# Feed-forward down projection by seven block products instead of eight in 9 of 11 units

## The chip, the core and the metric

One Trainium2 chip, one of its cores. The metric is the device time of one launch in microseconds (us), lower is better. Engines: TensorE (PE, with its weight loads as PEld), VectorE (DVE), ScalarE (ACT), GpSimd (POOL) and SyncE (SP), which issues the loads.

## The reference

Two blocks of two layers each over 256 tokens of width 1024. The first block (attention mixes and a mixture of experts) is not touched. A layer of the second block is

```
h = h + 0.5 * swiglu(rms_norm_2(h, ffn1_norm[l]), ffn1_w1[l], ffn1_w3[l], ffn1_w2[l])
h = h + token_mixer(...)
h = h + 0.5 * swiglu(rms_norm_2(h, ffn2_norm[l]), ffn2_w1[l], ffn2_w3[l], ffn2_w2[l])
swiglu(u, w1, w3, w2) = (silu(u @ w1) * (u @ w3)) @ w2      # w1, w3: 1024 x 2816, w2: 2816 x 1024
```

so there are four feed-forward parts. All data are 32-bit floats.

## The kernel before

**Products.** A 32-bit operand is split into a high part (rounded, by ScalarE) and a low part (the rest, by VectorE). `products` (L473 to L477) makes one product of a 128x128 stationary tile with a 128x512 moving tile by three matmuls: high by high (L475), high by low (L476), low by high (L477).

**A feed-forward part** is 11 units (`NU2`) of 256 hidden columns (`FE`). The tokens are two chunks of 128. A unit has three slabs of 128x2048 weights, held in a ring of three slots (`raw`, with `whi` and `wlo` for the split): two for the up and gate columns (k tiles 0 to 3 and 4 to 7) and one of `w2` for the down projection. TensorE does per unit: `unit_up`, 16 products for both chunks into banks 4 and 5; `unit_down`, 8 products (2 chunks by 2 halves of the columns by 2 k tiles) that accumulate over all units in banks 0 to 3 (`ybank`); `unit_transposes` (L903), four 128x128 transposes of the activation into bank 6. In the loop `unit_up` of unit u is followed by `unit_down` of unit u - 1 and by the transposes of unit u.

**The helpers.** ScalarE: `split_hi` of each slab in two halves (L464), silu of each chunk (L1630), `hi_part` of the transposed activation (L1640). VectorE: `split_lo` (L471), `activations` (L2058: gate times up), `lo_part` (L2063). At the end of a part `ffn_residual` adds half of each bank to x (L2466) and TensorE transposes x for the next stage (`transposes_h`, L1447) ahead of the last quarter of the last down projection; in the last part of all the final scaling follows (L2641).

**Order.** Each engine's program is written out by hand and run in order, and the engines are tied by counting semaphores: `slab_done` (TensorE is through with a slab), `hi_made` and `lo_made` (splits), `raw_in` (a load landed), `sg`, `a`, `aT`, `a_hi`, `a_lo` (the steps of the activation), `y_part`, `x_ready`. An engine that waits holds up all that is behind it on its own queue. `Fori` is a loop on the chip.

## Time and profile before

| | us |
|---|---|
| median of 3 runs (1526.9 to 1527.73) | 1527.6 |
| the profiled execution | 1526.78 |
| its span | 1525.0 |
| busy: PE / PEld / DVE / ACT / POOL | 1494.8 / 1142.2 / 828.7 / 716.2 / 98.3 |

The page gives each engine's busy time over the whole span, a strip of 40 slices, and the chain of work that ended last, of which 92% is TensorE. The four feed-forward parts lie at about 503 to 684, 825 to 1008, 1014 to 1195 and 1336 to 1515 us. The granted TensorE clock is 0.997 of full speed over the span.

### The profile page before, as it was taken

What the parts mean: (1) busy time and instruction counts of PE and PEld (TensorE: products, weight loads), DVE (VectorE), ACT (ScalarE), POOL (GpSimd) and SP (SyncE); (2) the same over time, 40 slices, a digit from 0 to 9 for tenths busy, and PEclk for the clock granted to TensorE, in tenths of its full rate; (3) what the DMA queues carried; (4) which work ended last, traced back from release to release, by engine and by line L of the source; (5) the groups of instructions that cost most, each with busy time, mean ns of one, the idle gap of its engine ahead of it and who ended that gap; (6) DMA issues with size and microseconds to landing.
All of it is one profiled execution on the core that took longest, in us unless ns stands there. A gap on an engine that the chain in (4) does not pass through costs nothing.

```text
span 1525.0 us, 20880 instructions
## 1 busy us (share of the span) xinstructions
PE 1494.8 (98%) x7748; PEld 1142.2 (75%) x7748; DVE 828.7 (54%) x1120; ACT 716.2 (47%) x1193; POOL 98.3 (6%) x166
## 2 busy tenths in 40 slices
PE   8999999999999999999999999999999999999998
PEld 7886335887433888888888888888888888888886
DVE  5675225576324655555766554565455566755544
ACT  5673223674213544445655444454444537454443
POOL 2321001231000000002000000000000100000000
PEclk9999999999999999999999999999999999999999
DMA  7739995547899555556345666656555643565551
GB/s 251 261 130 393 371 419 213 205 166 300 354 422 332 193 186 181 190 194 199 105 166 190 197 192 192 188 169 194 187 188 182 217 144 116 201 207 182 191 192 56
DMA packets 166054, 328.36 MB, mean 215 GB/s; under 512 B 8906, under 2 KB 106960, under 8 KB 153056
## 3 DMA queue, kind: packets, MB, share of 16 engines
q1 hardware_dynamic: 164992, 323.52, 60.7%
q0 software_dynamic: 992, 3.89, 0.9%
q8 instruction: 46, 0.75, 0.2%
q14 instruction: 24, 0.20, 0.0%
HBM read 326.33 MB, written 1.05 MB: 215 GB/s over the span
## 4 chain that ended last, share of the span: by engine, by line
PE 92%; DVE 3%; ACT 3%; DVEq 1%; issue 1%; DMA 1%; POOL 0%; SPq 0%; POOLq 0%; ACTq 0%
PE bank L475 24%; PE bank L477 23%; PE bank L476 23%; PE bank L1278 7%; PE bank L1327 4%; PE bank L903 1%; PE bank L1336 1%; PE bank L978 1%; DMA sb_raw<-w_in 1%; PE bank L1447 1%; PE bank L1069 1%; ACT sb_whi L464 1%; PE bank L1487 1%; PE bank L1515 0%; PE bank L1507 0%
## 5 line engine op out<-in xcount | busy, mean ns | idle before, releaser
L471 DVE TENSOR_TENSOR sb_wlo<-sb_raw,sb_whi 128x1024 fp32r<-128x1024 f32 (+1 forms) x417 | 479.9, 1194 | 321.8 <-ACT sb_whi L464 321.4
L464 ACT ACTIVATE sb_whi<-sb_raw 128x1024 fp32r<-128x1024 f32 (+2 forms) x419 | 408.1, 1028 | 295.5 <-PE bank L477 286.0
L475 PE MATMUL bank<-sb_whi,sb_op_hi 128*128 128x512 f32 (+2 forms) x1212 | 474.1, 391 | 3.4 <-DVE sb_op_lo L2089 1.7
L477 PE MATMUL bank<-sb_whi,sb_op_lo 128*128 128x512 f32 (+2 forms) x1212 | 466.3, 385 | 0.0
L476 PE MATMUL bank<-sb_wlo,sb_op_hi 128*128 128x512 f32 (+2 forms) x1212 | 465.5, 384 | 0.0
L475 PEld LDWEIGHTS bank<-sb_whi,sb_op_hi 128*128 128x128 f32 x1212 | 228.1, 188 | 49.9 <-issue 2.1
L477 PEld LDWEIGHTS bank<-sb_whi,sb_op_lo 128*128 128x128 f32 x1212 | 227.8, 188 | 45.9
L476 PEld LDWEIGHTS bank<-sb_wlo,sb_op_hi 128*128 128x128 f32 x1212 | 228.3, 188 | 42.4
L475 PE MATMUL bank<-sb_whi,sb_lat_hi 128*128 128x512 f32 (+2 forms) x456 | 175.7, 385 | 1.0 <-DVE sb_wlo L471 1.0
L477 PE MATMUL bank<-sb_whi,sb_lat_lo 128*128 128x512 f32 (+2 forms) x456 | 174.5, 383 | 0.0
L476 PE MATMUL bank<-sb_wlo,sb_lat_hi 128*128 128x512 f32 (+2 forms) x456 | 174.4, 382 | 0.0
L475 PEld LDWEIGHTS bank<-sb_whi,sb_lat_hi 128*128 128x128 f32 x456 | 85.6, 188 | 18.2 <-DVE sb_wlo L471 1.5
L477 PEld LDWEIGHTS bank<-sb_whi,sb_lat_lo 128*128 128x128 f32 x456 | 85.6, 188 | 16.3
L476 PEld LDWEIGHTS bank<-sb_wlo,sb_lat_hi 128*128 128x128 f32 x456 | 85.7, 188 | 15.9
L1630 ACT ACTIVATE sb_unit_work<-bank,sb_small 128x256 f32<-128x256 f32 x88 | 41.7, 474 | 115.8 <-PE bank L477 115.6
L2058 DVE SCALAR_TENSOR_TENSOR sb_unit_work<-bank,sb_small,sb_unit_work 128x256 f32<-128x256 f32 x88 | 42.4, 482 | 81.3 <-ACT sb_unit_work L1630 81.3
L1278 PE MATMUL bank<-sb_moe,sb_xg 128*64 128x512 f32 x288 | 70.9, 593 | 0.6 <-DVE sb_unit_work L2421 0.5
L2393 DVE TENSOR_TENSOR sb_unit_work<-bank,sb_unit_work 128x256 f32<-128x256 f32 x16 | 10.1, 631 | 100.8 <-ACT sb_unit_work L1873 100.8
L1873 ACT ACTIVATE sb_unit_work<-bank 128x256 f32<-128x256 f32 x16 | 6.1, 384 | 123.2 <-PE bank L1278 123.2
L778 POOL TENSOR_TENSOR sb_small<-sb_small,sb_half 128x2 f32<-128x2 f32 x5 | 3.5, 703 | 789.6 <-DVE sb_small L2455 789.6
L1278 PEld LDWEIGHTS bank<-sb_moe,sb_xg 128*64 128x64 f32 x288 | 22.3, 137 | 41.5 <-issue 40.0
L2063 DVE TENSOR_TENSOR sb_lat_lo<-bank,sb_lat_hi 128x512 fp32r<-128x512 f32 x44 | 30.2, 686 | 19.5 <-ACT sb_lat_hi L1640 19.5
(283 smaller groups left out, 1335.2 us busy)
## 6 DMA issues: line engine op xcount, KB each, us to landing
sb_raw<-ffn_w SPq DMA_DIRECT2D x264, 512.0 KB, 4.3
sb_raw<-w_in SPq DMA_DIRECT2D x84, 512.0 KB, 4.6
sb_moe<-exp_w_gate_up SPq DMA_DIRECT2D x36, 1024.0 KB, 11.9
sb_moe<-exp_w_down SPq DMA_DIRECT2D x18, 1024.0 KB, 11.5
sb_raw<-w_out SPq DMA_DIRECT2D x32, 512.0 KB, 4.3
sb_own<-exp_w_gate_up SPq DMA_DIRECT2D x12, 1024.0 KB, 8.5
sb_per_block<-exp_w_gate_up SPq DMA_DIRECT2D x4, 1024.0 KB, 4.9
sb_xg<-exp_w_gate_up SPq DMA_DIRECT2D x4, 1024.0 KB, 9.6
```

Of the source, the lines that this page charges most:

```text
L464: nc.scalar.activation(h, r, ACT.Copy).then_inc(hi_made.sem, 1)
L471: on.tensor_tensor(o, r, h.bitcast(F32), ALU.subtract).then_inc(lo_made.sem, 1)
L475: nc.tensor.matmul(ps, hi, wh, start=first, stop=False)
L476: nc.tensor.matmul(ps, hi, wl, start=False, stop=False)
L477: return nc.tensor.matmul(ps, lo, wh, start=False, stop=last)
L903: i = nc.tensor.transpose(bank[AB][:, f * T + ch * P:f * T + ch * P + P], av[:, ch, f * P:f * P + P], ident)
L978: i = nc.tensor.transpose(b[0:v.shape[1], n * T + ch * P:n * T + ch * P + P], v, ident)
L1278: i = nc.tensor.matmul(bank[4][r, :], xg[:, p // 4, 4 * h + k, o:o + CAP], w[e][:, 512 * k:512 * k + 512], start=h == 0 and k == 0, stop=h ...
L1327: i = nc.tensor.matmul(bank[6 + nh][r, :], pair_aT[:, p % 2, f, at:at + SEATS], w[e][:, o:o + 512], start=f == 0, stop=f == 1)
L1630: nc.scalar.activation(sg[:, ch, :], of(ch)[:, 0:FE], ACT.Silu, scale=1.0 if col is None else col(ch)).then_inc(S["sg"].sem, 1)
L2058: stt(out=av[:, ch, :], in0=of(ch)[:, FE:2 * FE], scalar=col(u, ch), in1=sg[:, ch, :], op0=ALU.mult, op1=ALU.mult).then_inc(S["a"].sem, 1)
L2063: tt(to.rearrange("p f t -> p (f t)"), bank[AB][:, :], hi.rearrange("p f t -> p (f t)").bitcast(F32), ALU.subtract).then_inc(S["a_lo"].sem, 1)
```

## The change

The down projection of a unit is a 2x2 by 2x2 block product: A (tokens by hidden columns, blocks of 128x128) times B (`w2`, blocks of 128x512). Units 1 to 9 make it by 7 products with sums of blocks, Winograd's form, in place of 8. For A, S1 = A21 + A22, S2 = S1 - A11, S3 = A11 - A21, S4 = A12 - S2; for B, T1 = B12 - B11, T2 = B22 - T1, T3 = B22 - B12, T4 = B21 - T2 in the signs of the code. The seven products accumulate over the nine units in seven banks (table `FAST`), and are put together once, at the end of the part. Units 0 and 10 keep 8 products.

Since seven banks are taken, the up projection of both chunks, and then the transposes, share bank 4: the up projection now runs chunk by chunk (`up_by_chunk`), with three of the products between the chunks, and the other four on both sides of the transposes. VectorE makes the sums of B (`weight_sums`, from `raw`), of A (`sums_of_a`), and the low parts of three sets: the two blocks of `w2` used as they are (`direct_lo`), the four sums of B and the seven blocks of A (`operands_lo`). ScalarE makes the high parts (`direct_hi`, `operands_hi`) and copies the transposes out of the bank (`turned_in`). SyncE loads a `w2` slab when `direct_lo` of the unit before is done. The diff, cut (lines of the code before that are replaced are shown in part):

```diff
+FAST = {1: (A11, (0, 0), None, 3), 2: (A12, (1, 0), None, 0), 3: (S4_OF_A, (1, 1), None, 1), 4: (A22, None, T4_OF_B, 2),
+5: (S1_OF_A, None, T1_OF_B, 7), 6: (S2_OF_A, None, T2_OF_B, 5), 7: (S3_OF_A, None, T3_OF_B, 6)}
...
+        def down_early(number, j, u):
+            slot, run = j % RING, j0 // S2_FFN2
+            wait_down = G["down_read"]
+            sp.wait_ge(wait_down.sem, wait_down.after(l, u + (run * NS - 1)))
...
+    def fast_down(slot, names, opening=False, closing=False):
+        for name in names:
+            of_a, direct, of_b, b = FAST[name]
+            w = tile(slot, D, 1, direct[0], 512 * direct[1], 512) if direct else (t_hi[:, of_b, :], t_lo[:, of_b, :])
+            i = products(bank[b][:, :], mix_a_hi[:, of_a - 1, :], mix_a_lo[:, of_a - 1, :], *w, opening, closing)
+        return i
...
+        up_by_chunk(S, l, num(j0 + 2), up_slot, 1, n0, lambda ch: bank[HB + ch], second_ready,
+                    lambda: unit_transposes(S, l, n0 + 1, first_up_bank(n0, 1), plain))
+        a_ready(1)
+        slab_ready(num(j0 + 4))
+        plain_down(down_slot, (1, 1), True, True)
+        plain_down(down_slot, (0, 0), True, False)
+        plain_down(down_slot, (0, 1), True, False)
+        unit_transposes(S, l, n0 + 2, bank[HB], mixed)
+        plain_down(down_slot, (1, 0), True, False).then_inc(slab_done.sem, 1)
...
+        def fast_unit(u, first):
+            def first_part():
+                a_ready(u)
+                fast_down(down_slot, (1,), first)
+                fast_down(down_slot, (2, 3)).then_inc(S["direct_done"].sem, 1)
             j = u * 3 + (j0 - 1)
-            unit_up(num(j), (j0 + 2) % RING, S["h_c0"], None, paired)
-            unit_down(S, l, num(j + 2), (j0 + 4) % RING, u + n0, by_chunk)
-            unit_transposes(S, l, 0, u + (n0 + 1))
-        j = j0 + 3 * count - 4
-        unit_up(num(j), (j0 + 2) % RING, S["h_c0"], None, paired)
-        unit_down(S, l, num(j + 2), (j0 + 4) % RING, n0 + count - 1, by_chunk[0:2], done=False)
-        unit_transposes(S, l, 0, n0 + count)
-        unit_down(S, l, num(j + 2), (j0 + 4) % RING, n0 + count - 1, by_chunk[2:4])
-        unit_down(S, l, num(j + 3), (j0 + 5) % RING, n0 + count, parts, True, last_hi, last_lo, S["y_part"], between=between)
+            up_by_chunk(S, l, num(j), up_slot, u, n0, lambda ch: bank[HB], up_ready(u), first_part)
+            slab_ready(num(j + 2))
+            fast_down(down_slot, (4,))
+            fast_down(down_slot, (5,), first)
+            unit_transposes(S, l, u + (n0 + 1), bank[HB], mixed)
+            fast_down(down_slot, (6, 7), first).then_inc(slab_done.sem, 1)
+        fast_unit(2, True)
+        with pe.Fori(3, count - 1) as u:
+            fast_unit(u, False)
+        u = count - 1
+        j = j0 + 3 * u - 1
+        def last_parts():
+            a_ready(u)
+            slab_ready(num(j + 2))
+            fast_down(down_slot, (1, 6, 7), closing=True)
+        up_by_chunk(S, l, num(j), up_slot, u, n0, lambda ch: bank[HB], up_ready(u), last_parts)
+        fast_down(down_slot, (5,), closing=True)
+        fast_down(down_slot, (2,))
+        unit_transposes(S, l, n0 + count, bank[HB], plain)
+        fast_down(down_slot, (3, 4)).then_inc(slab_done.sem, 1)
+        pe.sem_inc(S["direct_done"].sem, 1)
+        last_down(S, l, num(j + 3), (j0 + 5) % RING, n0 + count, parts, between)
...
+        with act.Fori(2, count - 1) as u:
+            operands_hi(u - 1)
+            silu(u, num(u * 3 + j0), (0,), one)
+            wait(S, "direct_done", l, u + (run * NS - 1))
+            direct_hi(u)
             ahead(j0 + 2, u)
-            silu(u, num(u * 3 + j0))
-        with act.Fori(1, count - 1) as u:
-            unit(u)
-            ahead(j0 + 3, u)
-            ahead(j0 + 4, u)
-        unit(count - 1)
-        hi_part(n0 + count, last_hi)
+            silu(u, num(u * 3 + j0), (1,), one)
+            ahead(j0 + 3, u, (0,))
+            turned_in(u, bank[HB])
+            ahead(j0 + 3, u, (1,))
...
+        def weight_sums(u):
+            dve.drain()
+            for i in range(2):
+                dve.wait_ge(raw_in[slot][i].sem, l * (16 * S2 // RING) + u * 16 + 16 * ((BASE2 + j0 + 4) // RING + 1))
+            b11, b12, b21, b22 = (raw[slot][:, o:o + 512] for o in range(0, SLAB, 512))
+            t1, t2, t3, t4 = (t_raw[:, i, :] for i in (T1_OF_B, T2_OF_B, T3_OF_B, T4_OF_B))
+            tt(t1, b12, b11, ALU.subtract)
+            tt(t3, b22, b12, ALU.subtract)
+            dve.drain()
+            tt(t2, b22, t1, ALU.subtract)
+            dve.drain()
+            tt(t4, b21, t2, ALU.subtract).then_inc(S["t_made"].sem, 1)
...
+        def operands_lo(u):
+            t_part(u, 0)
+            wait(S, "a_hi", l, u + (n0 + 1))
+            tt(mix_a_lo[:, :, :], a_parts[:, A11:S4_OF_A + 1, :], mix_a_hi[:, :, :].bitcast(F32), ALU.subtract).then_inc(S["a_lo"].sem, 1)
+            t_part(u, 1)
...
+        wait(S, "aT", l, n0 + 1)
+        activations(1, (0,))
+        last_lo_of(n0 + 1, first_up_bank(n0, 1))
+        activations(1, (1,))
+        ahead(j0 + 2, 1)
+        ahead(j0 + 3, 1, (0,))
+        weight_sums(1)
+        sums_of_a(1)
+        ahead(j0 + 3, 1, (1,))
+        slab_is_done(number(0))
+        halved(1, 1, bank[3][:, :])
+        direct_lo(1)
+        with dve.Fori(2, count - 1) as u:
+            operands_lo(u - 1)
+            activations(u, (0,), one)
+            weight_sums(u)
+            direct_lo(u)
             ahead(j0 + 2, u)
+            activations(u, (1,), one)
+            ahead(j0 + 3, u, (0,))
+            sums_of_a(u)
+            ahead(j0 + 3, u, (1,))
+        u = count - 1
+        operands_lo(u - 1)
+        activations(u, (0,), one)
+        slab_is_done(number(u - 1) - 2)
+        p1, u2, u3 = (joint[:, i, :] for i in range(3))
+        nc.vector.tensor_copy(p1, bank[3][:, :])
+        dve.drain()
+        tt(u2, bank[5][:, :], p1, ALU.add)
+        halved(0, 0, p1)
+        dve.drain()
+        tt(u3, bank[6][:, :], u2, ALU.add)
+        activations(u, (1,), one)
+        ahead(j0 + 2, u)
+        last_lo_of(n0 + count, bank[HB])
+        halved(0, 1, u2)
+        halved(1, 0, u3)
+        halved(1, 1, u3)
+        slab_is_done(number(u - 1))
+        dve.drain()
+        halved(0, 1, bank[7][:, :])
+        halved(1, 1, bank[7][:, :])
+        dve.drain()
```

In the order rows below bank and slot numbers stand behind the names, and the semaphores waited for in brackets. **VectorE at the start of a part**, from the activation of unit 0's second chunk on (L2058 and L2201 are `activations`; L471 and L483 `split_lo`; L2063 and L2250 the low part of the transposed activation). Before:

```order
L2058 SCALAR_TENSOR_TENSOR sb_unit_work<-bank2,sb_small,sb_unit_work 128x256 [waits g_sg]
L471 TENSOR_TENSOR sb_wlo0<-sb_raw0,sb_whi0 128x1024 [waits hi_made]
L471 TENSOR_TENSOR sb_wlo1<-sb_raw1,sb_whi1 128x1024 [waits hi_made] x2
L2076 UNCONDITIONAL_BRANCH
L2063 TENSOR_TENSOR sb_lat_lo<-bank6,sb_lat_hi 128x512 [waits g_a_hi]
L470 ISA
L471 TENSOR_TENSOR sb_wlo2<-sb_raw2,sb_whi2 128x1024 [waits hi_made]
```

After (L2214 to L2219 `weight_sums`, L2235 to L2240 `sums_of_a`):

```order
L2201 SCALAR_TENSOR_TENSOR sb_unit_work<-bank5,sb_small,sb_unit_work 128x256 [waits g_sg]
L483 TENSOR_TENSOR sb_wlo2<-sb_raw2,sb_whi2 128x1024 [waits hi_made] x2
L483 TENSOR_TENSOR sb_wlo0<-sb_raw0,sb_whi0 128x1024 [waits hi_made]
L2214 TENSOR_TENSOR sb_t_raw<-sb_raw1 128x512 [waits raw_in1_1,raw_in1_0]
L2215 TENSOR_TENSOR sb_t_raw<-sb_raw1 128x512
L2217 TENSOR_TENSOR sb_t_raw<-sb_raw1,sb_t_raw 128x512
L2219 TENSOR_TENSOR sb_t_raw<-sb_raw1,sb_t_raw 128x512
L2235 TENSOR_TENSOR sb_a_parts<-sb_a_parts 128x128 [waits g_a_in]
L2236 TENSOR_TENSOR sb_a_parts<-sb_a_parts 128x128
L2238 TENSOR_TENSOR sb_a_parts<-sb_a_parts 128x128
L2240 TENSOR_TENSOR sb_a_parts<-sb_a_parts 128x128
L483 TENSOR_TENSOR sb_wlo0<-sb_raw0,sb_whi0 128x1024 [waits hi_made]
```

Behind the last row stand `halved` (L2255), `direct_lo` (two rows of L2224), one row of L2230 and then L2245, the low parts of the seven blocks of A: 16 instructions come between the activation and it. **The loop**, on VectorE from the splits ahead of the second chunk's activation. Before:

```order
L470 REGISTER_ALU
L471 TENSOR_TENSOR sb_wlo2<-sb_raw2,sb_whi2 128x1024 [waits hi_made]
L2039 ISA
L2058 SCALAR_TENSOR_TENSOR sb_unit_work<-bank4,sb_small,sb_unit_work 128x256 [waits g_sg]
L2039 REGISTER_ALU
L2058 SCALAR_TENSOR_TENSOR sb_unit_work<-bank5,sb_small,sb_unit_work 128x256 [waits g_sg]
L470 ISA
L471 TENSOR_TENSOR sb_wlo0<-sb_raw0,sb_whi0 128x1024 [waits hi_made]
L470 REGISTER_ALU
```

After:

```order
L2219 TENSOR_TENSOR sb_t_raw<-sb_raw1,sb_t_raw 128x512
L2224 TENSOR_TENSOR sb_wlo1<-sb_raw1,sb_whi1 128x512 [waits g_direct_hi]
L2224 TENSOR_TENSOR sb_wlo1<-sb_raw1,sb_whi1 128x1024
L482 ISA
L483 TENSOR_TENSOR sb_wlo2<-sb_raw2,sb_whi2 128x1024 [waits hi_made]
L482 REGISTER_ALU
L483 TENSOR_TENSOR sb_wlo2<-sb_raw2,sb_whi2 128x1024 [waits hi_made]
L2182 REGISTER_ALU
L2201 SCALAR_TENSOR_TENSOR sb_unit_work<-bank4,sb_small,sb_unit_work 128x256 [waits g_sg]
L482 ISA
L483 TENSOR_TENSOR sb_wlo0<-sb_raw0,sb_whi0 128x1024 [waits hi_made]
L2235 TENSOR_TENSOR sb_a_parts<-sb_a_parts 128x128 [waits g_a_in]
```

The activation of chunk 1 (L2201) now stands behind both splits of the next unit's first slab (`wlo2`), and these behind the sums of B. On TensorE, the end of the loop's body. Before:

```order
L477 MATMUL bank3<-sb_whi1,sb_lat_lo 128x512
L475 MATMUL bank3<-sb_whi1,sb_lat_hi 128x512
L476 MATMUL bank3<-sb_wlo1,sb_lat_hi 128x512
L477 MATMUL bank3<-sb_whi1,sb_lat_lo 128x512
L900 ISA
L903 MATMUL bank6<-sb_const,sb_unit_work 128x128 [waits g_a]
L903 MATMUL bank6<-sb_const,sb_unit_work 128x128 x3
L943 REGISTER_ALU
L943 COMPARE_AND_BRANCH
```

After (L927 are the transposes):

```order
L489 MATMUL bank4<-sb_whi0,sb_op_lo 128x512
L839 ISA
L487 MATMUL bank2<-sb_t_hi,sb_mix_a_hi 128x512 [waits lo_made]
L488 MATMUL bank2<-sb_t_lo,sb_mix_a_hi 128x512
L489 MATMUL bank2<-sb_t_hi,sb_mix_a_lo 128x512
L487 MATMUL bank7<-sb_t_hi,sb_mix_a_hi 128x512
L488 MATMUL bank7<-sb_t_lo,sb_mix_a_hi 128x512
L489 MATMUL bank7<-sb_t_hi,sb_mix_a_lo 128x512
L836 ISA
L927 MATMUL bank4<-sb_const,sb_unit_work 128x128 [waits g_a]
L927 MATMUL bank4<-sb_const,sb_unit_work 128x128 x3
L487 MATMUL bank5<-sb_t_hi,sb_mix_a_hi 128x512
```

The transposes, which wait for the activation of chunk 1 (`g_a`), had 24 matmuls between them and the up projection, and have 6 now; 6 more stand between them and the next up projection, which waits for the bank to be copied out (`g_a_in`). **VectorE at the end of a part.** Before:

```order
L471 TENSOR_TENSOR sb_wlo2<-sb_raw2,sb_whi2 128x1024 [waits hi_made] x2
L2058 SCALAR_TENSOR_TENSOR sb_unit_work<-bank4,sb_small,sb_unit_work 128x256 [waits g_sg]
L2058 SCALAR_TENSOR_TENSOR sb_unit_work<-bank5,sb_small,sb_unit_work 128x256 [waits g_sg]
L2063 TENSOR_TENSOR sb_lat_lo<-bank6,sb_lat_hi 128x512 [waits g_a_hi]
L471 TENSOR_TENSOR sb_wlo0<-sb_raw0,sb_whi0 128x1024 [waits hi_made] x2
L2466 SCALAR_TENSOR_TENSOR sb_x<-bank0,sb_x 128x512 [waits g_y_part]
L2466 SCALAR_TENSOR_TENSOR sb_x<-bank2,sb_x 128x512 [waits g_y_part]
L2466 SCALAR_TENSOR_TENSOR sb_x<-bank1,sb_x 128x512 [waits g_y_part]
```

After:

```order
L2292 COPY sb_joint<-bank3 128x512 [waits slab_done]
L2294 TENSOR_TENSOR sb_joint<-bank5,sb_joint 128x512
L2255 SCALAR_TENSOR_TENSOR sb_x<-sb_joint,sb_x 128x512
L2297 TENSOR_TENSOR sb_joint<-bank6,sb_joint 128x512
L2201 SCALAR_TENSOR_TENSOR sb_unit_work<-bank4,sb_small,sb_unit_work 128x256 [waits g_sg]
L483 TENSOR_TENSOR sb_wlo2<-sb_raw2,sb_whi2 128x1024 [waits hi_made] x2
L2250 TENSOR_TENSOR sb_lat_lo<-bank4,sb_lat_hi 128x512 [waits g_a_hi]
L2255 SCALAR_TENSOR_TENSOR sb_x<-sb_joint,sb_x 128x512 x3
L2255 SCALAR_TENSOR_TENSOR sb_x<-bank7,sb_x 128x512 [waits slab_done]
L2255 SCALAR_TENSOR_TENSOR sb_x<-bank7,sb_x 128x512
L483 TENSOR_TENSOR sb_wlo0<-sb_raw0,sb_whi0 128x1024 [waits hi_made] x2
L2692 SCALAR_TENSOR_TENSOR sb_x<-bank0,sb_x 128x512 [waits g_y_part]
```

The rows ISA and REGISTER_ALU compute the counts waited for. Four steps of putting together stand ahead of the last activation, the splits of the last slab ahead of the last low part (L2250), and five more steps (L2255) between that and the splits and residuals (L2692) of the next stage.

## Rows read from the trace of the kernel before

**Rows 1.** The page: span, busy time, and loads (KB each, us to landing)

```profile
span 1525.0 us, 20880 instructions
...
PE 1494.8 (98%) x7748; PEld 1142.2 (75%) x7748; DVE 828.7 (54%) x1120; ACT 716.2 (47%) x1193; POOL 98.3 (6%) x166
...
sb_raw<-ffn_w SPq DMA_DIRECT2D x264, 512.0 KB, 4.3
```

**Rows 2.** Groups by form, VectorE: out<-in xcount, busy us, mean ns, idle before

```profile
L471 DVE TENSOR_TENSOR sb_wlo<-sb_raw,sb_whi 128x1024 fp32r<-128x1024 f32 x393 | 464.6, 1225 | 311.9 <-ACT sb_whi L464 311.5
L2058 DVE SCALAR_TENSOR_TENSOR sb_unit_work<-bank,sb_small,sb_unit_work 128x256 f32<-128x256 f32 x88 | 42.4, 482 | 81.3 <-ACT sb_unit_work L1630 81.3
L2063 DVE TENSOR_TENSOR sb_lat_lo<-bank,sb_lat_hi 128x512 fp32r<-128x512 f32 x44 | 30.2, 686 | 19.5 <-ACT sb_lat_hi L1640 19.5
L2331 DVE TENSOR_TENSOR sb_unit_work<-sb_unit_work,sb_const 128x128 f32<-128x128 f32 x2 | 0.6, 292 | 0.1
```

**Rows 3.** Groups by form, ScalarE

```profile
L464 ACT ACTIVATE sb_whi<-sb_raw 128x1024 fp32r<-128x1024 f32 x395 | 395.5, 1054 | 293.3 <-PE bank L477 283.8 <-DMA sb_raw<-w_in 6.6 <-DMA sb_raw<-ffn_w 2.9
L1630 ACT ACTIVATE sb_unit_work<-bank,sb_small 128x256 f32<-128x256 f32 x88 | 41.7, 474 | 115.8 <-PE bank L477 115.6
L1640 ACT ACTIVATE sb_lat_hi<-bank 128x512 fp32r<-128x512 f32 x44 | 25.6, 581 | 24.7 <-PE bank L903 24.7
```

**Rows 4.** Timeline of TensorE over one unit: start, duration, instruction

```profile
1360.97 0.60 PE L903 MATMUL bank<-sb_const,sb_unit_work 128*128 128x128 f32 x4
...
1366.88 0.39 PE L475 MATMUL bank<-sb_whi,sb_op_hi 128*128 128x512 f32 x1
...
1372.32 0.39 PE L475 MATMUL bank<-sb_whi,sb_lat_hi 128*128 128x512 f32 x1
...
1377.76 0.60 PE L903 MATMUL bank<-sb_const,sb_unit_work 128*128 128x128 f32 x4
```

**Rows 5.** Timeline of ScalarE in the same unit

```profile
1367.16 2.01 ACT L464 ACTIVATE sb_whi<-sb_raw 128x1024 fp32r<-128x1024 f32 x2 [3.49 <-PE bank L477]
...
1372.52 0.47 ACT L1630 ACTIVATE sb_unit_work<-bank,sb_small 128x256 f32<-128x256 f32 x1 [2.25 <-PE bank L477]
```

**Rows 6.** Timeline of VectorE in the same unit

```profile
1368.25 2.36 DVE L471 TENSOR_TENSOR sb_wlo<-sb_raw,sb_whi 128x1024 fp32r<-128x1024 f32 x2 [3.03 <-ACT sb_whi L464]
1370.53 0.48 DVE L2058 SCALAR_TENSOR_TENSOR sb_unit_work<-bank,sb_small,sb_unit_work 128x256 f32<-128x256 f32 x1
1373.03 0.49 DVE L2058 SCALAR_TENSOR_TENSOR sb_unit_work<-bank,sb_small,sb_unit_work 128x256 f32<-128x256 f32 x1 [2.02 <-ACT sb_unit_work L1630]
```

**Rows 7.** Timeline, start of the mixer's last stage: TensorE waits for VectorE's second split

```profile
1318.04 3.50 DVE L471 TENSOR_TENSOR sb_wlo<-sb_raw,sb_whi 128x1024 fp32r<-128x1024 f32 x3
...
1320.45 0.50 PE L475 MATMUL bank<-sb_whi,sb_op_hi 128*128 128x512 f32 x1
...
1320.79 0.39 PE L476 MATMUL bank<-sb_wlo,sb_op_hi 128*128 128x512 f32 x1
```

**Rows 8.** Timeline of VectorE at the end; a drain stands ahead of L2641

```profile
1514.15 0.69 DVE L2466 SCALAR_TENSOR_TENSOR sb_x<-bank,sb_x 128x512 f32<-128x512 f32 x1 [2.86 <-PE bank L477]
1514.94 0.69 DVE L2641 TENSOR_TENSOR sb_proj<-sb_x,sb_table 128x512 f32<-128x512 f32 x1
1515.55 0.68 DVE L2466 SCALAR_TENSOR_TENSOR sb_x<-bank,sb_x 128x512 f32<-128x512 f32 x1
```

**Rows 9.** Timeline of VectorE at the start of the fourth part

```profile
1344.89 0.49 DVE L2058 SCALAR_TENSOR_TENSOR sb_unit_work<-bank,sb_small,sb_unit_work 128x256 f32<-128x256 f32 x1 [0.25 <-ACT sb_unit_work L1630]
1345.29 3.49 DVE L471 TENSOR_TENSOR sb_wlo<-sb_raw,sb_whi 128x1024 fp32r<-128x1024 f32 x3
```

**Rows 10.** Timelines of VectorE and TensorE at the end of the first part

```profile
676.47 2.36 DVE L471 TENSOR_TENSOR sb_wlo<-sb_raw,sb_whi 128x1024 fp32r<-128x1024 f32 x2 [0.26 <-ACT sb_whi L464]
679.00 0.69 DVE L2466 SCALAR_TENSOR_TENSOR sb_x<-bank,sb_x 128x512 f32<-128x512 f32 x1 [0.17 <-PE bank L477]
...
681.52 1.03 PE L1447 MATMUL bank<-sb_const,sb_x 128*128 128x128 f32 x8
```

184 lines of the change are left out of this document (138 added, 46 removed).

## The prediction

> **What bounds the kernel now.** I read the page first: TensorE is busy for 1494.8 of 1525.0 us and VectorE for 54% [rows 1], so fewer matmuls can shorten the time, and nothing else can by much. Then the timeline of TensorE over a unit of the feed-forward loop: 24 matmuls start between 1366.88 and 1372.32, so one costs 0.2267 us whatever its own duration of 0.39, and from transposes to transposes it is 16.79 us, which is 72 x 0.2267 = 16.32 and 0.47 for the four transposes [rows 4]. No wait is left in it: the unit is matmuls alone. The same unit on ScalarE and VectorE [rows 5, 6] gives the delays from one engine to the next, and the groups by form [rows 2, 3] the prices.
>
> **What goes.** Nine units of four parts lose one block product, three matmuls: 36 x 3 x 0.2267 = 24.5 us, all on the path, as far as TensorE goes on without waits. 6.12 us of it fall to each part. The rest of this section is whether it does.
>
> **Prices on VectorE.** A split of 128x1024 follows another after 2.36 - 1.22 = 1.14 us [rows 2, 6], an activation takes 0.48 and lets the next start after 0.40. A 128x512 step takes 0.69 and the next starts 0.61 after its start (1514.94 to 1515.55); with a drain between it is 0.79 (1514.15 to 1514.94), so a drain costs 0.18 [rows 8]. For steps on 128x128 I take 0.29 [rows 2] less the same overlap, 0.21. The 128x896 step has no row; it lies between 0.69 and 1.22, and by the slope between these two it is 1.09. Per unit of the loop I add: six 1024-wide steps 6.84 and one of the same width in `direct_lo` 1.14, five of 512 (four sums, one direct) 3.05, the 896 step 1.01, two activations 0.80, four small sums 0.84, five drains 0.90: 14.6 us, in a unit that would last 69 x 0.2267 + 0.47 = 16.1. It fits, but VectorE has 1.5 us left where it had 8.5 (before: six splits, one 512 step, two activations), and its order decides. ScalarE carries about 10 us [rows 3] and is not the limit. The loads are the same bytes, 4.3 us from issue to landing [rows 1], and each is issued over 10 us ahead of its use; I cost SyncE at nothing. If a load were late by more than these 5 us, the splits behind it would slip by as much.
>
> A drain by the page of the Trainium skill, VectorE: DVE Perf Modes, section "The DRAIN you can't avoid", would be nothing extra, since by its account the next step waits for the pipe to empty anyhow. The trace does not agree (0.61 without, 0.79 with) [rows 8]; with drains free the start of a part below would be 0.9 us shorter and its end 0.36, and the sum 5.0 us less.
>
> **Start of a part.** Count from the start of unit 1's up projection. TensorE: 24 matmuls 5.44, transposes 0.47, 24 more to 11.35, 18 of the plain down projection to 15.43, transposes and 6 more to 17.26. It wants the second slab of unit 2 at 19.98, and the operands of the first seven products at 22.70. VectorE in the part before the change is here at its splits early [rows 9], and now waits for the second activation of unit 1: TensorE to ScalarE 0.20, silu 0.47 [rows 4, 5], and 0.04 on to VectorE [rows 5, 6], 12.06. From there one queue: activation 0.40, three splits 3.42, sums of B 4 x 0.61 + 3 x 0.18 = 2.98, sums of A 4 x 0.21 + 2 x 0.18 = 1.20, to 20.06; the fourth split ends 21.28. A late start costs TensorE 0.16 more (where it waited for VectorE's second split, that ended at 1318.04 + 1.14 + 1.22 = 1320.40, TensorE started at 1320.45, and its second matmul came 0.34 after, not 0.23 [rows 7]): it starts at 21.44, **1.46 late**. Then `halved` 0.61, `direct_lo` 0.61 + 1.14, one t part 1.14, the 896 step 1.09: 21.20 + 4.59 = 25.79, and TensorE starts at 25.95 against 22.70 + 1.46: **1.79 late**. Together 3.25 a part, 13.0 us in all. Bounds: with drains at nothing 2.35 a part, at twice the row 4.15.
>
> **The loop.** The transposes want the activation of chunk 1. Before, 24 matmuls hid it; now 6 do. Ahead of it VectorE must split the first slab of the next unit, which ScalarE can only begin when TensorE is through with that slab, halfway in chunk 1. By rows of the unit before: TensorE's slab ends at 1366.88, ScalarE starts at 1367.16, VectorE at 1368.25, the activation behind the two splits ends at 1370.53 + 0.48 = 1371.01: 4.13 us [rows 4, 5, 6]. TensorE has 12 + 6 matmuls meanwhile, 4.08. With the 0.16 of a late start it waits 4.13 + 0.16 - 4.08 = **0.21 a unit**. Eight units (2 to 9) of four parts: 6.7 us. This needs VectorE free when the first high part is made, 11.57 us into the unit; by the prices above it is (activation of chunk 0 at 6.15, then 0.40, the sums 2.98 with the drain ahead, direct 0.61 + 1.14: 11.3), with 0.3 to spare. The other waits have room: the second slab is split at 2.0 (wanted 2.7), the low parts of A are there at 4.2 (wanted 5.4), those of the sums of B at 5.3 (wanted 12.9), and the bank is copied out 0.6 before the next unit wants it. Bounds: 0.13, where ScalarE takes up in 0.20 as it does for the silu [rows 4, 5], and 0.5, where drains cost 0.3.
>
> **End of a part.** In unit 10, counted from its start, TensorE has its transposes at 14.3 and wants the last low part at 16.11. VectorE: the copy and three sums of the banks from 10.4, done by 13.2; activation from 13.63; two splits of the last slab from 14.03 to 16.31; the low part ends at 17.00. With 0.16: **1.05 late**, 4.2 in all. Then VectorE puts together five more: 16.91 + 3 x 0.61 + 0.18 + 2 x 0.61 + 0.18 = 20.32, where before it went from the low part straight to the splits [rows 10]. Two splits to 22.60, two residuals (0.61 + 0.69) to 23.90. TensorE, 18 matmuls on from 17.16, is at the transposes of x at 21.24, and starts at 24.06: 2.8 late, less 0.1 since a first pair of them waits for one residual only. **2.7**, in three parts. In the trace before they did not wait [rows 10]. In the fourth part there are no splits; the last residual starts at 20.32 + 3 x 1.40 + 0.15 instead of just behind the last matmul, about 1.6 more. End in all 4.2 + 8.1 + 1.6 = 13.9.
>
> **Sum.** -24.5 + 13.0 + 6.7 + 13.9 = +9.1 us on the profiled execution of 1526.78, so 1535.9. The median of the runs lies 0.8 above that execution; I say 1536, a slower kernel by 0.6%.
>
> **Rivals.** *One: VectorE's queue at the two ends is no gate.* The place is the chain of 13.7 us at the start and of 6.8 at the end, which I added up from spacings between other instructions [rows 6, 8]. If at both ends TensorE found its operands ready, 27 of the 33.6 us would go: 1526.8 - 24.5 + 6.7 = 1509. It turns the sign where the waits of a part come to less than 6.12; my rows give 8.4. Against it: every row of a 512-wide step with two tensors says 0.69, and no piece of the queue may be passed. For it: only that such seams are the least certain part of a hand count. *Two: the loop is bound by VectorE.* It has 0.3 us to spare ahead of the splits; each 0.1 us beyond that is 3.2 us in 32 units. Drains at 0.36 or a count computed for each wait in the loop that shows (0.08 by ScalarE's 0.28 against 0.20 [rows 4, 5]) would make it 0.3 to 0.6 a unit more: 1546 to 1555. *Three: a milder case.* Waits of 0.05 a unit and drains that cost nothing take 5.1 and 5.0 off: 1527 for the median, no difference that can be told. *That the change does not do what it says:* only if the new order ran as many matmuls; the rows of the order say 69 a unit.
>
> **Chances.** The forecast (1531 to 1544) 0.57, rival two 0.15, rival three 0.17, rival one 0.11. A measurement of this kernel can tell about 0.2%, 3.1 us, from no change. Faster 0.11, same 0.17, slower 0.72. The range leaves out most of rival one and the far end of rival two: 1524 to 1549.
>
> **What would show it.** Right: the page's matmuls (PE) at 108 fewer and idle time of TensorE up by over 25 us; transposes 16.3 us apart in the loop; in the first 30 us of a part two waits of TensorE of 1 to 2 us, one for a split and one for the 896-wide step; at the end a wait of 1 us for the last low part and one of 2 to 3 ahead of the transposes of x. Wrong: transposes at 16.1 apart (no loop wait) or over 16.5 (rival two); ends without waits (rival one); a wait of an engine for a load.

## The result, and the profile after

The changed kernel takes 1543.8 us (median of 5 runs, 1542.6 to 1546.0), the kernel before, run beside it, 1527.3: ratio 1.0111, 95% interval 1.0099 to 1.0122. It is slower by 16.5 us; I had forecast 9.1. The page of the changed kernel, its span and busy times:

```profile
span 1541.9 us, 21231 instructions
...
PE 1487.6 (96%) x7640; PEld 1120.4 (73%) x7640; DVE 1057.4 (69%) x1520; ACT 806.1 (52%) x1301; POOL 98.4 (6%) x166
```

Against [rows 1]: 108 matmuls fewer, as forecast. TensorE's idle time grows from 30 to 54 us, by 24.1, a little less than the "over 25" that was named as a sign. Its losses add up to 41 us (the 24.5 of the matmuls saved and the 16.9 by which the span grew); the rest of them counts as busy, a slower pace of the matmuls among it. VectorE goes from 54 to 69%. What TensorE waits for is best asked of its waits (us in total, times, longest); in the kernel before none of its ten largest waits was inside a feed-forward part:

```profile
PE bank L1548 <- DVE sb_x L2692: 6.3, 6, 2.1
PE bank L487 <- DVE sb_mix_a_lo L2245: 5.7, 4, 1.5
PE bank L487 <- DVE sb_wlo L483: 5.5, 6, 1.1
PE bank L927 <- DVE sb_unit_work L2201: 4.3, 4, 1.2
PE bank L487 <- DVE sb_lat_lo L2250: 2.9, 4, 0.7
```

Five waits for VectorE. Four of them stand in the prediction (transposes of x, low parts of A, split of unit 2's second slab, last low part). The fourth line does not: TensorE's transposes in unit 2 wait for the activation, once a part. All five in the timeline of TensorE in the first part; the other parts look the same:

```profile
504.66 0.50 PE L487 MATMUL bank<-sb_whi,sb_op_hi 128*128 128x512 f32 x1 [0.23 <-DVE sb_op_lo L2325]
...
531.50 0.50 PE L487 MATMUL bank<-sb_whi,sb_op_hi 128*128 128x512 f32 x1 [1.12 <-DVE sb_wlo L483]
...
535.97 0.50 PE L487 MATMUL bank<-sb_whi,sb_mix_a_hi 128*128 128x512 f32 x1 [1.42 <-DVE sb_mix_a_lo L2245]
...
546.38 0.66 PE L927 MATMUL bank<-sb_const,sb_unit_work 128*128 128x128 f32 x4 [1.19 <-DVE sb_unit_work L2201]
562.79 0.66 PE L927 MATMUL bank<-sb_const,sb_unit_work 128*128 128x128 f32 x4
579.19 0.66 PE L927 MATMUL bank<-sb_const,sb_unit_work 128*128 128x128 f32 x4
...
680.24 0.50 PE L487 MATMUL bank<-sb_whi,sb_lat_hi 128*128 128x512 f32 x1 [0.72 <-DVE sb_lat_lo L2250]
...
684.23 0.39 PE L489 MATMUL bank<-sb_whi,sb_lat_lo 128*128 128x512 f32 x1
686.45 0.44 PE L1548 MATMUL bank<-sb_const,sb_x 128*128 128x128 f32 x2 [1.83 <-DVE sb_x L2692]
687.04 0.88 PE L1548 MATMUL bank<-sb_const,sb_x 128*128 128x128 f32 x6 [0.16 <-DVE sb_x L2692]
687.67 0.48 PE L487 MATMUL bank<-sb_whi,sb_lat_hi 128*128 128x512 f32 x1
```

The parts, each measured from its first matmul behind the transposes of x to the same place of the next stage, were 184.1, 186.9, 186.9 and (to the end) 189.1 us and are 188.4, 191.2, 191.0 and 192.3: +15.8. The other 1.1 of the spans' 16.9 lies ahead of the first part, in code that was not changed; over the kernels below that leave it alone, that point lies anywhere between 502.9 and 505.3.

The unit 2 wait starts in SyncE's queue. VectorE and ScalarE there, and SyncE's own issues (columns as in the other timelines):

```profile
531.96 1.82 DVE L2224 TENSOR_TENSOR sb_wlo<-sb_raw,sb_whi 128x512 fp32r<-128x512 f32 x2
...
539.10 0.69 DVE L2214 TENSOR_TENSOR sb_t_raw<-sb_raw 128x512 f32<-128x512 f32 x1 [1.65 <-DMA sb_raw<-ffn_w]
...
543.58 2.35 DVE L483 TENSOR_TENSOR sb_wlo<-sb_raw,sb_whi 128x1024 fp32r<-128x1024 f32 x2
545.86 0.47 DVE L2201 SCALAR_TENSOR_TENSOR sb_unit_work<-bank,sb_small,sb_unit_work 128x256 f32<-128x256 f32 x1
...
541.22 1.07 ACT L476 ACTIVATE sb_whi<-sb_raw 128x1024 fp32r<-128x1024 f32 x1 [1.13 <-DMA sb_raw<-ffn_w]
...
533.98 0.88 SPq L642 DMA_DIRECT2D sb_raw<-ffn_w  x2
```

The load of unit 2's down slab may only start when `direct_lo(1)` is through with the slab (531.96 + 1.82 = 533.78). It is issued at 533.98, and VectorE starts on it at 539.10. Behind it the queue of VectorE has no gap up to the activation at 545.86.

### The profile page after: what moved, and what is told of

It is laid out like the page before. It is cut to its first block, busy times and chain, and to the rows that moved or that the text cites. A ratio compares the mean times of both kernels' runs of the same rounds, so it can differ in the third digit from the quotient of the medians.

```text
span 1541.9 us, 21231 instructions
## 1 busy us (share of the span) xinstructions
PE 1487.6 (96%) x7640; PEld 1120.4 (73%) x7640; DVE 1057.4 (69%) x1520; ACT 806.1 (52%) x1301; POOL 98.4 (6%) x166
## 4 chain that ended last, share of the span: by engine, by line
PE 83%; DVE 8%; ACT 3%; DVEq 2%; DMA 2%; issue 2%; POOL 0%; SPq 0%; POOLq 0%; ACTq 0%
PE bank L487 21%; PE bank L489 20%; PE bank L488 20%; PE bank L1379 7%; PE bank L1428 4%; DVE sb_wlo L483 2%; PE bank L927 1%; DMA sb_raw<-ffn_w 1%; PE bank L1437 1%; DVE sb_wlo L2224 1%; PE bank L1079 1%; DVE sb_x L2255 1%; DMA sb_raw<-w_in 1%; PE bank L1548 1%; PE bank L1170 1%
## 5 line engine op out<-in xcount | busy, mean ns | idle before, releaser
L483 DVE TENSOR_TENSOR sb_wlo<-sb_raw,sb_whi 128x1024 fp32r<-128x1024 f32 (+3 forms) x345 | 397.2, 1187 | 111.1 <-ACT sb_whi L476 110.4
L476 ACT ACTIVATE sb_whi<-sb_raw 128x1024 fp32r<-128x1024 f32 (+3 forms) x347 | 339.1, 1023 | 123.8 <-PE bank L489 111.7
L2230 DVE TENSOR_TENSOR sb_t_lo<-sb_t_raw,sb_t_hi 128x1024 fp32r<-128x1024 f32 x72 | 87.7, 1217 | 0.0
L2201 DVE SCALAR_TENSOR_TENSOR sb_unit_work<-bank,sb_small,sb_unit_work 128x256 f32<-128x256 f32 x88 | 42.3, 481 | 63.2 <-ACT sb_unit_work L1731 63.2
L1749 ACT ACTIVATE sb_t_hi<-sb_t_raw 128x1024 fp32r<-128x1024 f32 x72 | 75.7, 1052 | 0.0
L487 PE MATMUL bank<-sb_whi,sb_lat_hi 128*128 128x512 f32 (+2 forms) x168 | 64.2, 382 | 3.9 <-DVE sb_lat_lo L2250 2.9
L2224 DVE TENSOR_TENSOR sb_wlo<-sb_raw,sb_whi 128x512 fp32r<-128x512 f32 x72 | 65.5, 951 | 0.0
L489 PE MATMUL bank<-sb_whi,sb_lat_lo 128*128 128x512 f32 (+2 forms) x168 | 62.4, 372 | 0.0
L488 PE MATMUL bank<-sb_wlo,sb_lat_hi 128*128 128x512 f32 (+2 forms) x168 | 62.4, 371 | 0.0
L487 PE MATMUL bank<-sb_t_hi,sb_mix_a_hi 128*128 128x512 f32 x144 | 59.5, 413 | 0.0
L489 PE MATMUL bank<-sb_t_hi,sb_mix_a_lo 128*128 128x512 f32 x144 | 57.2, 397 | 0.0
```

Of the source, the lines that this page charges most:

```text
L476: nc.scalar.activation(h, r, ACT.Copy).then_inc(hi_made.sem, 1)
L483: on.tensor_tensor(o, r, h.bitcast(F32), ALU.subtract).then_inc(lo_made.sem, 1)
L487: nc.tensor.matmul(ps, hi, wh, start=first, stop=False)
L488: nc.tensor.matmul(ps, hi, wl, start=False, stop=False)
L489: return nc.tensor.matmul(ps, lo, wh, start=False, stop=last)
L1749: nc.scalar.activation(t_hi[:, 2 * part:2 * part + 2, :], t_raw[:, 2 * part:2 * part + 2, :], ACT.Copy).then_inc(hi_made.sem, 1)
```

## Experiments

**Start of a part.** One call, the four sums of B of unit 1, moved on VectorE:

```diff
                 last_lo_of(n0 + 1, first_up_bank(n0, 1))
+                weight_sums(1)
                 activations(1, (1,))
                 ahead(j0 + 2, 1)
                 ahead(j0 + 3, 1, (0,))
-                weight_sums(1)
                 sums_of_a(1)
```

> The four sums of B of unit 1 (`weight_sums(1)`) are moved on VectorE from behind the three splits to ahead of unit 1's second activation, where VectorE idles 4.65 us in the trace of the changed kernel; nothing else is changed. Theory (VectorE's queue is the gate at the start of a part): the queue behind the activation is 3.1 us shorter. TensorE's wait for the second slab's split (1.28 us late) goes; the one for the low parts of A (1.59 late) shrinks to about 0.85, since three splits, the sums of A, direct_lo and two more steps still stand in a row. About 2.1 us a part, 8.5 in all: 1535.3, against 1543.8 of the changed kernel and 1527.3 of the one before. The wait of 1.3 to 1.6 us of unit 2's transposes stays. Rival (the starts are gated by ScalarE's high parts or by loads, and VectorE's lateness is only their echo): 1543 to 1544.

Measured 1537.0 us (the kernel before, run beside it, 1526.5; ratio 1.0067, 1.0050 to 1.0084), 6.8 less than the changed kernel. Its TensorE:

```profile
532.59 0.50 PE L487 MATMUL bank<-sb_whi,sb_mix_a_hi 128*128 128x512 f32 x1 [0.73 <-DVE sb_mix_a_lo L2245]
542.92 0.66 PE L927 MATMUL bank<-sb_const,sb_unit_work 128*128 128x128 f32 x4 [1.12 <-DVE sb_unit_work L2201]
```

The wait for the split is gone, the other is 1.12 from the matmul before it instead of 1.81, as worked out. VectorE's queue was the gate. Of my 8.5, 1.7 are missing: the wait of unit 2 grew by 0.1 on the mean, and at two of the ends of a part TensorE ran at the lower clock for 3 us (below).

**Unit 2.** SyncE's order:

```diff
+                up(slab_number(BASE2, S2, l, j0 + 8), j0 + 2, 3)
+                down_early(slab_number(BASE2, S2, l, j0 + 10), j0 + 4, 2)
-                with sp.Fori(3, NU2) as u:
+                with sp.Fori(4, NU2) as u:
                     j = u * 3 + (j0 - 1)
                     down_early(slab_number(BASE2, S2, l, j + 2), j0 + 4, u - 1)
                     up(slab_number(BASE2, S2, l, j), j0 + 2, u)
```

> SyncE's order alone: the loads of unit 3's two up slabs are issued ahead of the load of unit 2's down slab, which has to wait for unit 1's direct_lo; from unit 3 on the order is that of the changed kernel. It tells apart what makes TensorE wait 1.3 to 1.6 us at the transposes of unit 2, once a part, which I had not predicted. In that trace two loads are late there: the down slab of unit 2 (VectorE idles 1.65 for it ahead of its sums) and the first up slab of unit 3, stuck behind it in SyncE's queue (ScalarE idles 1.13 and 0.44 for it). Theory A (the down slab's load is the cause: VectorE goes from its landing through sums, direct_lo and two splits without a gap of its own, 6.8 us): no gain, 1543.5 to 1544.1, the wait stays within 0.1. Theory B (the up slab held behind it is the cause): the wait goes, 1.3 a part, 1538.5.

Measured 1543.9 (ratio 1.0116, 1.0099 to 1.0133): no change. ScalarE no longer waits for a load there, only for TensorE, and still the transposes wait, 1.53 to 1.77 us from the matmul before them where it was 1.34 to 1.59:

```profile
540.44 2.01 ACT L476 ACTIVATE sb_whi<-sb_raw 128x1024 fp32r<-128x1024 f32 x2 [1.15 <-PE bank L489]
...
538.30 0.69 DVE L2216 TENSOR_TENSOR sb_t_raw<-sb_raw 128x512 f32<-128x512 f32 x1 [1.60 <-DMA sb_raw<-ffn_w]
...
545.59 0.66 PE L929 MATMUL bank<-sb_const,sb_unit_work 128*128 128x128 f32 x4 [1.13 <-DVE sb_unit_work L2203]
```

The up slab was late as well and cost nothing. What is left is the down slab's load, 1.6 us late for VectorE, that TensorE gets to feel 7 us later. That it is the cause is read from VectorE's queue, which has no gap in between; no run moved this load alone.

**The loop.**

```diff
                     direct_lo(u)
-                    ahead(j0 + 2, u)
+                    ahead(j0 + 2, u, (0,))
                     activations(u, (1,), one)
+                    ahead(j0 + 2, u, (1,))
```

> In the loop alone: VectorE makes the activation of chunk 1 between the two halves of the next slab's split instead of behind both. The period in the changed kernel is 16.40 us, 0.29 over the 16.11 of 69 matmuls at 0.2267 and four transposes. Theory (mixed): only 0.06 of wait and 0.06 to 0.1 of late start are due to the activation; the rest is that the 21 matmuls with the mixed tiles of A run at 0.2333 apart instead of 0.2267 (0.14 a unit), which no order of VectorE changes. With the activation between the halves VectorE makes it 0.2 earlier, just in time: period 16.26 to 16.28, 3.5 to 4 us in all, 1540. Rival (my prediction's account: the whole 0.29 is the wait for the activation): period 16.11 to 16.2, 6.4 to 9.3 us in all, 1534.5 to 1537.4. Second rival (it is ScalarE's silu that sets it): 1543.8.

Measured 1541.5 (ratio 1.0100, 1.0084 to 1.0117), 2.3 less, where 3.5 to 4 were expected; the intervals of the two ratios overlap, so the rows have to carry this. Three readings. The period falls by 0.07 only, to 16.33, half of what was expected, and no wait is left in it:

```profile
544.14 0.65 PE L927 MATMUL bank<-sb_const,sb_unit_work 128*128 128x128 f32 x4
560.51 0.60 PE L927 MATMUL bank<-sb_const,sb_unit_work 128*128 128x128 f32 x4
576.84 0.60 PE L927 MATMUL bank<-sb_const,sb_unit_work 128*128 128x128 f32 x4
```

The wait of unit 2 is gone too, since there also the activation now comes one split earlier (0.9 to 1.25 us a part, which I had not expected of this edit). And 0.4 a part comes back in unit 10, where two products wait for a low part of the sums of B that VectorE now makes later. In sum 0.9 to 1.3 a part up to the transposes of x (in the last part, up to the end), 4.3 in all; about half of it is lost again behind them, at the lower clock. The granted clock in windows over the end of the first part (stretch: length, busy times, then the clock, DMA share, GB/s):

```profile
680.00:684.00 4.00, 2.36 (x11) 1.63 (x9) 3.92 (x5) 0.29 (x1) 0.00 (x0) 1.00 0.86 327
684.00:686.00 2.00, 1.65 (x9) 1.42 (x9) 1.33 (x3) 0.49 (x2) 0.00 (x0) 0.71 1.05 376
686.00:688.20 2.20, 2.20 (x7) 1.78 (x6) 1.73 (x4) 1.19 (x3) 0.00 (x0) 0.50 0.75 286
688.20:691.00 2.80, 2.80 (x14) 2.28 (x13) 2.32 (x3) 0.00 (x0) 0.00 (x0) 0.99 0.00 1
```

**End of a part.** TensorE signals the closing of three banks, VectorE puts together in its idle time, and the first residuals go ahead of the next splits (the core of the edit):

```diff
-                    fast_down(down_slot, (1, 6, 7), closing=True)
+                    fast_down(down_slot, (1, 6, 7), closing=True).then_inc(S["direct_done"].sem, 1)
...
-                slab_is_done(number(u - 1) - 2)
+                wait(S, "direct_done", l, u + (run * NS - 1))
...
-                activations(u, (1,), one)
                 ahead(j0 + 2, u)
+                activations(u, (1,), one)
+                halved(0, 1, u2)
+                dve.drain()
+                halved(1, 0, u3)
                 last_lo_of(n0 + count, bank[HB])
-                halved(0, 1, u2)
-                halved(1, 0, u3)
                 halved(1, 1, u3)
-                slab_is_done(number(u - 1))
...
-                following(3)
-                ffn_residual(0, num(S2_Q - 1), by_half, range(3))
+                ffn_residual(0, num(S2_Q - 1), by_half, range(2))
+                following(3)
+                ffn_residual(0, num(S2_Q - 1), by_half, (2,))
```

> The end of a part alone. TensorE signals the closing of banks 3, 5 and 6 right behind their last product, so that VectorE puts them together in the 3.9 us in which it idles ahead of its copy; the splits of the last slab, the activation, one half and the last low part follow; bank 7 is added without a wait for the last product; and in the next stage the first two residuals stand ahead of the splits. Theory (VectorE's queue at the end of a part is the gate, 1.05 + 2.7 a part and 1.05 + 1.6 in the last): the wait for the last low part shrinks from 0.9 to 0.1 to 0.3, the one at the transposes of x from 2.4 to under 0.3, the last residual starts just behind the last matmul: 3 x 3.0 + 2.3 = 11.3 us less, 1532.5. Rival (the splits or residuals moved behind turn into a wait of the next stage's first matmuls, and half of it comes back): 1538.

Measured 1534.2 (ratio 1.0049, 1.0032 to 1.0065), 9.6 less. Its VectorE and TensorE:

```profile
670.37 0.69 DVE L2291 COPY sb_joint<-bank 128x512 f32<-128x512 f32 x1 [1.10 <-PE bank L489]
...
683.31 1.03 PE L1547 MATMUL bank<-sb_const,sb_x 128*128 128x128 f32 x8
...
686.63 0.47 PE L487 MATMUL bank<-sb_whi,sb_op_hi 128*128 128x512 f32 x1 [0.92 <-DVE sb_op_lo L2674]
```

Both waits at the end go, and in the last part the time from the last matmul to the end falls from 8.8 to 7.5 us (7.3 before the change). Part of the rival comes true: three times TensorE waits 1.1 us more for the low parts of the next stage's operand, which now stand behind two splits and a residual. So 9.6 of the 11.3 expected.

**The address of the mixed tiles.** Most of what was left in the loop was no wait but pace. In the changed kernel nine matmuls of the products take 2.10 us from the first to the matmul behind them, 0.2333 each, where the matmuls of a unit before the change took 0.2267 [rows 4]:

```profile
570.15 0.39 PE L487 MATMUL bank<-sb_whi,sb_mix_a_hi 128*128 128x512 f32 x1
...
572.25 0.40 PE L487 MATMUL bank<-sb_whi,sb_op_hi 128*128 128x512 f32 x1
```

In the built program `op_hi`, all slabs and the split sums of B (`t_hi`, `t_lo`) begin 128 bytes behind a multiple of 512 of their partition, `mix_a_hi` and `mix_a_lo` 480. The first test is a gap of 32 bytes ahead of them, which puts them on a multiple of 512:

```diff
         with ExitStack() as fast:
             t_raw = fast.enter_context(nc.sbuf_tensor("sb_t_raw", [P, 4, 512], F32))
+            fast.enter_context(nc.sbuf_tensor("sb_gap", [P, 8], F32))
             a_parts = fast.enter_context(nc.sbuf_tensor("sb_a_parts", [P, 8, P], F32))
```

> Nothing but an address: a gap of 32 bytes is put ahead of a_parts, so that the mixed tiles of A (mix_a_hi, mix_a_lo), the stationary side of the seven products, begin on a multiple of 64 bytes of their partition, as op_hi and lat_hi do; in the changed kernel they begin on 200672 and 204256, which are multiples of 32 only. Theory: that is what makes the 21 matmuls of the products start 0.2333 us apart in the loop instead of 0.2267. They go back to 0.2267: 756 x 0.0066 = 5.0 us less, 1538.8, and the period of the loop goes from 16.40 to 16.24 or so. Rival (the order of the banks, or moving tiles of two kinds, makes them slower): the pitch stays at 0.2333 and the time at 1543.8.

Measured 1542.7 (ratio 1.0104, 1.0087 to 1.0121): 1 us, which the spread of the runs does not tell from nothing, and not 5. The period is 16.38. The up projection's matmuls behind the products go to 0.2267, the 21 products stay at 0.2333 on the mean. As a theory of multiples of 64 it has fallen. The second test is the kernel before, with its own stationary tiles moved by 32 bytes, to 160 behind a multiple of 512:

```diff
+        cur1 = sb("cur1", [P, 7])
         op_hi = sb("op_hi", [P, DK, T], F32R)
         op_lo = sb("op_lo", [P, DK, T], F32R)
...
-        cur1 = sb("cur1", [P, 7])
```

> The kernel before, with one small tile (cur1, 28 bytes) allocated ahead of op_hi instead of behind cols, so that op_hi, op_lo, lat_hi and lat_lo, the stationary sides of the feed-forward matmuls, begin 32 bytes off a multiple of 64; no instruction is changed. Theory of the address: the 72 matmuls of each of 44 units start 0.2333 apart, the loop's period goes from 16.79 to 17.26, 44 x 72 x 0.0066 = 20.9 us in the four parts, and with the other stages that use these tiles 25 to 40 in all: 1552 to 1567. Rival (addresses do not matter): 1526 to 1528 and 16.79.

Measured 1555.3 (ratio 1.0178, 1.0161 to 1.0195): 28 us from an address, with the same instructions and a granted clock of 1.00 in both kernels over 560 to 580 us (`const`, `per_block`, `table`, `rows_of` and `cols` moved along; the products do not read them). The transposes are 17.25 apart, (17.25 - 16.79) / 72 = 0.0064 a matmul:

```profile
549.24 0.60 PE L903 MATMUL bank<-sb_const,sb_unit_work 128*128 128x128 f32 x4
566.49 0.60 PE L903 MATMUL bank<-sb_const,sb_unit_work 128*128 128x128 f32 x4
```

To tell the place from the products themselves, the products got another stationary side (this kernel computes something else), and then the mixed tiles another place:

```diff
-                    i = products(bank[b][:, :], mix_a_hi[:, of_a - 1, :], mix_a_lo[:, of_a - 1, :], *w, opening, closing)
+                    i = products(bank[b][:, :], op_hi[:, of_a - 1, 0:P], op_lo[:, of_a - 1, 0:P], *w, opening, closing)
```

> The changed kernel with one thing exchanged: the seven products of units 1 to 9 take tiles of op_hi and op_lo as their stationary side instead of mix_a_hi and mix_a_lo, so that the down projection of these units computes something else; same banks, same moving tiles, same waits, same count. Having the mixed tiles on a multiple of 64 bytes left their matmuls at 0.2341 apart (though the matmuls of the up projection behind them went from 0.2310 to 0.2267). Theory A (it is where the mixed tiles lie): all 69 matmuls of a unit at 0.2267, period 16.24. Theory B (it is the products themselves: seven banks changed every three matmuls, or the waits and register steps between them): still 0.233 or more for the 21, period 16.40.

```diff
+            fast.enter_context(nc.sbuf_tensor("sb_gap", [P, 40], F32))
             a_parts = fast.enter_context(nc.sbuf_tensor("sb_a_parts", [P, 8, P], F32))
```

> The changed kernel with a gap of 160 bytes instead of 32 ahead of a_parts: the mixed tiles begin 128 bytes behind a multiple of 512, as op_hi, lat_hi and all slabs do, where the gap of 32 put them on a multiple of 512. If what counts is a multiple of 64 alone: as with the gap of 32, the products' 21 matmuls 0.2341 apart, period 16.38. If the mixed tiles must lie like the other stationary tiles to be read at their pace: 0.2267 and a period of 16.24, about 4 us less.

Both have 0.2267 for all products and a period of 16.26 on the mean: 1541.2 (ratio 1.0088, 1.0068 to 1.0108) and 1542.3 (1.0095, 1.0075 to 1.0115). The second one's TensorE:

```profile
570.39 0.39 PE L488 MATMUL bank<-sb_whi,sb_mix_a_hi 128*128 128x512 f32 x1
...
572.43 0.39 PE L488 MATMUL bank<-sb_whi,sb_op_hi 128*128 128x512 f32 x1
```

Nine in 2.04 us. It is the place. The times gained less (2.6 and 1.5) than the 4.6 us that the rows give (in each of four parts seven units of 0.14, and 0.18 in unit 10); in the profiles two and three ends of a part run at the lower clock, for 1.1 to 1.25 us each. And which place: the kernel before, its tiles 64 bytes on, at 192 behind a multiple of 512.

```diff
+        sinks = sb("sinks", [P, DEPTH, SWH])
         op_hi = sb("op_hi", [P, DK, T], F32R)
...
-        sinks = sb("sinks", [P, DEPTH, SWH])
```

> The kernel before, with one small tile of 64 bytes (sinks) allocated ahead of op_hi: op_hi, op_lo, lat_hi and lat_lo begin 192 bytes behind a multiple of 512, on a multiple of 64 but 64 bytes away from where the slabs (the moving side) begin. It asks which rule of address the pitch follows. If a multiple of 64 were enough: 0.2267 and 16.79 as before, 1527. If the stationary tile has to lie at the slabs' 128 behind 512 (or on a multiple of 128): 0.2333 and 17.24, as with a shift of 32, near 1555. The mixed tiles on a multiple of 512 were slow (0.2333), so I lean to the second.

Measured 1553.3 (ratio 1.0172, 1.0151 to 1.0192), period 17.23. So of the places tried 128 behind 512 is fast and 0, 160, 192 and 480 are slow (0 and 480 with the mixed tiles, 160 and 192 with the others). Since the moving side lies at 128 behind 512 in every kernel, these runs do not tell whether the stationary side has to be there or just where the moving side is.

**All together.** The edits so far, unit 1's `direct_lo` ahead of `halved`, the low parts of A ahead of those of the sums of B, and in unit 10 a wait for the first pair of those sums only:

```diff
-                    t_part(u, 0)
                     wait(S, "a_hi", l, u + (n0 + 1))
                     tt(mix_a_lo[:, :, :], a_parts[:, A11:S4_OF_A + 1, :], mix_a_hi[:, :, :].bitcast(F32), ALU.subtract).then_inc(S["a_lo"].sem, 1)
+                    t_part(u, 0)
                     t_part(u, 1)
...
-                    slab_ready(num(j + 2))
+                    pe.wait_ge(lo_made.sem, num(j + 2) * 2 + (1 + 2 * RING))
...
+                following(3, (0,))
+                operand_lo_k(1, TPB, (0, 1))
+                following(3, (1,))
```

> All that the single experiments point to, in one kernel that computes the same as the changed one: unit 1's sums of B made early; at the start direct_lo ahead of the half of bank 3; the low parts of A ahead of those of the sums of B (on ScalarE their high parts likewise); the activation of chunk 1 between the two splits; the end as in the experiment on the end, with the low parts of the next operand between the two halves of the next split; in unit 10 a wait for the first half of the sums of B only; and the address of the mixed tiles. Theory (each of these is a gate of its own, and nothing is queued behind them): TensorE's waits of a part fall from about 9.6 us to 1.5, the loop's period to 16.15, and of the 24.5 us of matmuls some 18 are kept: 1506 to 1511, faster than the kernel before by 1.0 to 1.3%. Rival (VectorE, with 13 of 16 us taken in the loop, turns each wait removed into the next one): 1520 or more.

Measured 1524.0 (ratio 0.9978, 0.9968 to 0.9987): the rival's time. Three causes, two of them in these rows of its TensorE:

```profile
533.85 0.50 PE L488 MATMUL bank<-sb_whi,sb_op_hi 128*128 128x512 f32 x1 [0.30 <-DVE sb_unit_work L2202]
...
682.44 0.50 PE L488 MATMUL bank<-sb_whi,sb_op_hi 128*128 128x512 f32 x1 [1.92 <-DVE sb_wlo L484]
```

In unit 2 the up projection waits 0.5 a part for the activation of chunk 0, which stands behind the low parts of all sums of B. The next stage needs its slab split in full, so putting the low parts between the halves was wrong and costs 2.1 us three times. And the pace of the loop (16.36) was still that of the slow address. Mended in two steps, first the waits (the core of the edit):

```diff
-                following(3, (0,))
-                operand_lo_k(1, TPB, (0, 1))
-                following(3, (1,))
-                ffn_residual(0, num(S2_Q - 1), by_half, (2, 3))
+                ffn_residual(0, num(S2_Q - 1), by_half, (0,))
+                following(3, (0,))
+                ffn_residual(0, num(S2_Q - 1), by_half, (1,))
+                following(3, (1,))
+                operand_lo_k(1, TPB, (0, 1))
+                ffn_residual(0, num(S2_Q - 1), by_half, (2, 3))
...
                     t_part(u, 0)
+                    activations(u + 1, (0,), lambda ch: bank[HB])
                     t_part(u, 1)
```

> The kernel with all edits, two of them mended by its trace: the next stage's slab has to be split in full before its first matmul (TensorE waited 2.1 us there, three times, with the second half put behind the low parts of its operand), so now the two halves stand between the first two residuals and right behind them, and the third residual behind the operand's low parts; and the activation of chunk 0 stands between the low parts of the two pairs of sums of B, for which chunk 1 of unit 2 waited 0.47. Theory (these were waits of their own, 6.3 and 1.9 us): 1515 to 1518. Rival (moved on again): 1521 or more. The period of the loop stays at 16.35, since none of its 0.25 over 16.11 is a wait.

Measured 1515.0 (ratio 0.9918, 0.9902 to 0.9935), as expected. Then the place of the mixed tiles, the gap 40 wide instead of 8:

> The kernel with all edits (waits at both ends, unit 2, the order in the loop), and the gap ahead of the mixed tiles 160 bytes instead of 32, so that they begin 128 bytes behind a multiple of 512, like the other stationary tiles. The gap of 160 alone took the products' matmuls from 0.2333 to 0.2267 apart and the loop's period from 16.40 to 16.26 in a kernel with 0.1 of wait left in the loop. Theory (pitch and waits add up): period 16.13 to 16.18 instead of 16.31 here, 32 x 0.15 = 4.8 us less than 1515.0: 1509 to 1512, faster than the kernel before by 1.0 to 1.2%. Rival (with TensorE faster, VectorE or ScalarE becomes late in the loop, and a wait takes the place of the slower pitch): 1513 to 1516 and a period above 16.25 with waits of TensorE in it.

Measured 1512.2 (ratio 0.9904, 0.9888 to 0.9921), 14.9 us or 1.0% faster than the kernel before, with these transposes. It gained 2.8 of the 4.8 expected:

```profile
541.40 0.66 PE L928 MATMUL bank<-sb_const,sb_unit_work 128*128 128x128 f32 x4 [0.61 <-DVE sb_unit_work L2202]
557.65 0.60 PE L928 MATMUL bank<-sb_const,sb_unit_work 128*128 128x128 f32 x4
573.76 0.60 PE L928 MATMUL bank<-sb_const,sb_unit_work 128*128 128x128 f32 x4
589.91 0.60 PE L928 MATMUL bank<-sb_const,sb_unit_work 128*128 128x128 f32 x4
```

16.15 apart, 0.04 above 69 matmuls and four transposes; unit 2 keeps a wait of 0.6 to 0.7. In the third part it is 16.24, with a slower pace in the first chunk of the up projection and two waits of 0.5 at its start; why there alone stays open.

## Why the prediction was right or wrong

Its steps with what the two traces show. A wait is taken as the time from the matmul before it less 0.23, with 0.11 for the slow second matmul behind it; four parts. In the row of unit 2 the 0.23 is taken off in one sum, 0.9.

| term | predicted | measured |
|---|---|---|
| 108 matmuls fewer | -24.5 | -24.5 |
| start: split, low parts of A | 13.0 | 4 x (1.39 + 1.69) = 12.3 |
| unit 2: late load | 0 | 1.59 + 1.34 + 1.52 + 1.45 - 0.9 = 5.0 |
| loop | 6.7 | 4 x (7 x 0.29 + 0.23) = 9.0 |
| last low part | 4.2 | 4 x 1.00 = 4.0 |
| transposes of x | 8.1 | 2.4 + 2.7 + 2.4 = 7.5 |
| end of the last part | 1.6 | 8.78 - 7.27 = 1.5 |
| sum | +9.1 | +14.8 |

The parts grew by 15.8. The remaining 1.0 is about what the slower pace of the products of units 1 and 10 would cost (8 x 0.14); no run takes it apart.

**Right: what bounds, and both ends.** The chain of 16 VectorE steps at the start gave 13.0 for 12.3 and those at the end 13.9 for 13.0, within 7%. Rival one (no gate at the ends) is excluded by the experiments on start and end: each edit touched only VectorE's order and signals for it, and the waits it was aimed at went, or shrank by what was worked out. VectorE's spacings are close to those of the sum:

```profile
526.35 0.69 DVE L2214 TENSOR_TENSOR sb_t_raw<-sb_raw 128x512 f32<-128x512 f32 x1 [0.17 <-issue]
526.96 0.68 DVE L2215 TENSOR_TENSOR sb_t_raw<-sb_raw 128x512 f32<-128x512 f32 x1
527.71 0.69 DVE L2217 TENSOR_TENSOR sb_t_raw<-sb_raw,sb_t_raw 128x512 f32<-128x512 f32 x1
528.48 0.69 DVE L2219 TENSOR_TENSOR sb_t_raw<-sb_raw,sb_t_raw 128x512 f32<-128x512 f32 x1
```

0.61 without a drain, 0.75 and 0.77 with one: a drain costs 0.15 here, 0.18 in [rows 8], and not nothing. So the account of the Trainium skill, VectorE: DVE Perf Modes, section "The DRAIN you can't avoid", does not hold for these as the prediction read it.

**Wrong: the loads at nothing.** The step that failed is "each is issued over 10 us ahead of its use; I cost SyncE at nothing". It holds in the loop, where `direct_lo` ends at 576.16 and the next sums begin at 588.00. It does not hold for unit 2: I had put `direct_lo(1)` at the end of the very queue that I found late, and did not carry on to who waits for its end. 533.78 plus 5.3 for the load is 539.1; the sums would have begun at 537.45. The 4.3 us a load that the prediction took from the trace before is short as well, for with its other order of issues the changed kernel has 5.3 in the median:

```profile
sb_raw<-ffn_w SPq DMA_DIRECT2D x264, 512.0 KB, 5.3
```

The text named a late load as what would make it wrong, and asked for 5 us of lateness; 1.65 of waiting were enough, because VectorE has next to no slack in its chain to the activation (the 0.3 that the text itself gives).

**The loop: size near, account wrong.** 0.21 a unit was forecast as a wait for the activation. Measured are 0.29, of which the address of the stationary tiles makes 0.14 (16.40 to 16.26 by the address alone). The late activation makes 0.13 by the rows: the transposes start 0.30 behind the matmul before them and not 0.23, and the matmul behind them starts 0.41 after them, 0.35 where they are in time. The loop's edit took both away and gained only 0.07, for the matmuls of the unit then went 0.2303 apart on the mean, where it had been 0.2296. So pace and wait are not independent; why, no run shows. Rival two (VectorE bounds the loop) is not what happened: VectorE waits 0.22 for ScalarE ahead of these splits in every unit, and with all waits removed the loop runs at 16.15 with the same steps on it.

```profile
576.38 2.36 DVE L483 TENSOR_TENSOR sb_wlo<-sb_raw,sb_whi 128x1024 fp32r<-128x1024 f32 x2 [0.22 <-ACT sb_whi L476]
```

So the direction came from the two ends, which were right. That the time fell within the range was partly luck: 1543.8 lies 0.2 us under its upper end of 1544. The missing 7 us are a load that I let go as covered (5.0) and a pace that the prediction did not foresee (4 to 5), less overestimates of the two ends (1.6) and of the wait in the loop.

## What to carry to other kernels

When an engine's queue is found late somewhere, follow everything that it issues or releases at that point, the load that waits for its last step above all: the lateness comes back one load time later, at a place that looks unrelated. Work that replaces matmuls by steps of other engines pays when these steps stand where the engine idles; here the same seven products are 1.1% slower or 1.0% faster than eight, by the order on VectorE, a few signals and the address of two tiles. After new tiles are allocated, compare TensorE's pitch over ten matmuls with the old one before looking for waits.

## What the runs showed of the hardware

The start address of the stationary tile changes TensorE's pitch: 0.2267 us a 128x512 matmul with both sides 128 bytes behind a multiple of 512, 0.2333 with the stationary side 0, 160, 192 or 480 behind it, over thousands of matmuls and with no instruction changed (28 us of 1527 in the kernel before). The Trainium skill, TensorE: Matmul & The Clock Gate, section "Step-by-step: what each phase is for", has the next tile's load and the running matmul on two read ports that do not disturb each other. By that the pitch should not depend on where the stationary tile lies; the trace does not agree. The address is not the only thing that slows the pitch: with tiles at the fast place it is also 0.231 to 0.233 for stretches of 2 to 5 us, often behind a wait. In the kernel before, ten matmuls behind the wait of [rows 7] take from 1320.79 to 1323.10. What makes these stretches was not tested.

TensorE's clock fell to its lower level (matmuls 0.43 apart, granted clock 0.50) at the transposes of x in some executions, for about 3 us, after 1 us of wait for the last low part and 2.2 to 2.5 for x: at two ends in the experiments on the start and on the loop, at two and three in those on the products' stationary side and its place, at none in the changed kernel's own profile, which has the same waits. That is the level of 1.2 GHz of the two, 1.2 and 2.4. Such a spell makes the way from these transposes to those of the next stage 6.3 to 6.5 us long instead of 5.2, so it costs 1.1 to 1.25. In the first kernel with all edits there is one, behind its wait of 2.3 for a split. Where these waits were removed (the end's experiment, and the last two kernels) none occurs. What decides between the executions was not found.
